# Which engine makes the low halves of the recurrence's split weights: VectorE and GpSimd in turn, or VectorE alone

## What is computed

```python
z = jnp.einsum('bld,de->ble', h, w_in)
x_lru, g_lru, u_s5, gate_a, gate_b = jnp.split(z, SPLITS, axis=-1)
y_a = jax.nn.gelu(g_lru) * rg_lru(causal_depthwise_conv(x_lru, conv_w, conv_b), wa, ba, wx, bx, lam)
y_a = jnp.einsum('blr,rd->bld', y_a, w_lru_out)
y_s = jax.nn.gelu(s5_ssm(u_s5, a_re, a_im, b_re, b_im, c_re, c_im, d, log_dt))
```

## Time and profile before

| | |
|---|---|
| median of 3 runs | 1433.82 us (1431.03 to 1434.45) |
| the profiled execution | 1432.98 us, span 1431.2 us |
| PE busy | 1367.4 us, 96% of the span |
| DVE busy | 968.1 us, 68% |
| ACT busy | 697.3 us, 49% |
| POOL busy | 458.4 us, 32% |
| the four rounds of the recurrence | about 94 to 371 us |

### The profile page before, as it was taken

One profiled execution on the slowest core, in us unless ns is written; L12 is line 12 of the kernel. 1 busy time (PEld: TensorE's weight loads), 2 busy tenths in 40 slices (PEclk: granted clock), 3 DMA queues, 4 the chain that ended last, 5 costly groups with the idle time before them and its releaser, 6 DMA issues.

```text
span 1431.2 us, 19574 instructions
## 1 busy us (share of the span) xinstructions
PE 1367.4 (96%) x6615; PEld 980.0 (68%) x6615; DVE 968.1 (68%) x1429; ACT 697.3 (49%) x994; POOL 458.4 (32%) x361
## 2 busy tenths in 40 slices
PE   7979999999899999999999999999999999999991
PEld 6867778777788888884545666666666666666660
DVE  6788977786511111648626888888778787887875
ACT  4225655647422222210024666676666666676661
POOL 0002432316444444000010433334343355554430
PEclk9989999999999999999999999999999999999996
DMA  9044253534232334741058999999999999999974
GB/s 259 7 128 74 75 75 83 96 63 109 80 100 84 96 104 138 296 169 46 0 202 317 352 367 362 364 365 373 364 371 365 368 371 371 371 366 369 370 226 132
DMA packets 140918, 315.82 MB, mean 221 GB/s; under 512 B 18128, under 2 KB 99712, under 8 KB 115456
## 3 DMA queue, kind: packets, MB, share of 16 engines
q1 hardware_dynamic: 126528, 281.50, 56.5%
q0 software_dynamic: 14336, 33.59, 9.9%
HBM read 297.27 MB, written 34.54 MB: 232 GB/s over the span
## 4 chain that ended last, share of the span: by engine, by line
PE 71%; DMA 11%; DVE 9%; ACT 3%; issue 2%; DVEq 2%; POOL 1%; SPq 1%; ACTq 0%; POOLq 0%
PE bank L723 17%; PE bank L725 16%; PE bank L724 16%; DMA gate_up<-moe_w_up_in 9%; PE bank L1105 5%; PE bank L730 5%; DVE arena L1440 4%; PE bank L892 3%; DVEq L1437 2%; PE bank L970 2%; DVE arena L1446 2%; PE bank L990 1%; ACT arena L1170 1%; ACT gate_up_high L1170 1%; PE bank L1064 1%
## 5 line engine op out<-in xcount | busy, mean ns | idle before, releaser
L1440 DVE TENSOR_TENSOR gate_up_low<-gate_up,gate_up_high 128x1024 fp32r<-128x1024 f32 x256 | 296.6, 1221 | 93.7 <-ACT gate_up_high L1170 93.7
L1170 ACT ACTIVATE gate_up_high<-gate_up 128x1024 fp32r<-128x1024 f32 x256 | 249.7, 1049 | 90.8 <-DMA gate_up<-moe_w_up_in 90.6
L1170 ACT ACTIVATE arena<-bank 96x512 f32<-96x512 f32 (+5 forms) x244 | 128.8, 553 | 250.4 <-PE bank L725 119.2
L672 POOL DMA_INDIRECT acc_dram<-arena x64 | 117.6, 1838 | 317.9 <-DMA acc_dram<-arena 286.1
L723 PE MATMUL bank<-gate_up_high,rows_high 128*96 128x512 f32 x512 | 206.1, 403 | 4.9 <-DVE rows_low L1440 4.9
L1440 DVE TENSOR_TENSOR arena<-arena 128x512 f32<-128x512 f32 (+12 forms) x288 | 194.9, 710 | 15.3 <-ACT arena L1170 3.2
L725 PE MATMUL bank<-gate_up_high,rows_low 128*96 128x512 f32 x512 | 202.6, 396 | 0.0
L724 PE MATMUL bank<-gate_up_low,rows_high 128*96 128x512 f32 x512 | 200.9, 392 | 0.0
L730 PEld LDWEIGHTS bank<-arena 96*128 96x128 f32 (+5 forms) x1001 | 126.5, 186 | 54.1 <-issue 38.2
L599 POOL TENSOR_TENSOR wb_low<-arena,wb_high 128x1024 fp32r<-128x1024 f32 (+1 forms) x40 | 106.7, 2673 | 144.5 <-ACT wb_high L1170 144.5
L730 PE MATMUL bank<-arena 96*128 96x96 f32 (+5 forms) x1001 | 126.6, 265 | 7.9 <-DMA arena<-x_in 4.8
(11 more groups left out here) (171 smaller groups left out, 2586.2 us busy)
## 6 DMA issues: line engine op xcount, KB each, us to landing
gate_up<-moe_w_gate_in SPq DMA_DIRECT2D x64, 1024.0 KB, 18.2
gate_up<-moe_w_up_in SPq DMA_DIRECT2D x64, 1024.0 KB, 21.2
down<-moe_w_down_in SPq DMA_DIRECT2D x64, 1024.0 KB, 16.0
arena<-w_in_in SPq DMA_DIRECT2D x40, 512.0 KB, 4.1
arena<-w_glu_in SPq DMA_DIRECT2D x16, 512.0 KB, 3.9
arena<-w_lru_out_in SPq DMA_DIRECT2D x8, 768.0 KB, 4.7
arena<-x_in SPq DMA_DIRECT2D x8, 512.0 KB, 5.2
wu<-w_in_in SPq DMA_DIRECT2D x8, 512.0 KB, 8.2
```

Of the source, the lines that this page charges most:

```text
L672: nc.gpsimd.indirect_dma_start(out=acc_dram, out_offset=bass.IndirectOffsetOnAxis(ap=idxcol[:, 4 + c:5 + c].bitcast(u32), axis=0), in_=yb[ ...
L1170: return nc.scalar.activation(out_, in_, func, **kw)
L1440: return V_.tensor_tensor(out_, a, b_, op)
```

## The change

Every low part of the x and g weights goes to VectorE. GpSimd loses its twelve (x tiles 0 and 1, g tiles 1 and 2, in three rounds each). On VectorE the low parts of g tiles 1 and 2 stand right behind the convolution of the tile with that number in every round (until now in round 0 only), and those of the next round's x tiles 0, 1 and 2 stand behind `tables_in` (until now tile 2 only). TensorE now waits for them by one count, `v_split`. Waits for `w_split` in the products behind the rounds are renumbered.

```diff
             for b in range(NB):
-                for m in range(1, ML if b else 1):
-                    low_part(wa[m], wa_lo[m], wa_hi[m], ML * (2 * b + 1) + m)
 
                 pool.wait_ge(S["RT_put"], 4 * (b + 1))
                 pool.wait_ge(S["U_put"], 2 * (b + 1))
...
                 pool.sem_inc(S["K_kept"], 1)
-                if b + 1 < NB:
-                    for m in range(2):
-                        low_part(wa[m], wa_lo[m], wa_hi[m], ML * (2 * b + 2) + m)
-                else:
+                if b + 1 == NB:
                     low_b(0)
                     low_b(1)
...
             def x_proj(b, m):
-                if b == 0:
-                    pe.wait_ge(S["v_split"], m + 1)
-                elif m < 2:
-                    pe.wait_ge(S["w_split"], 4 * b + m - 3)
-                else:
-                    pe.wait_ge(S["v_split"], 2 * b + 5)
+                pe.wait_ge(S["v_split"], 2 * ML * b + m + 1)
...
-                    if b == 0:
-                        pe.wait_ge(S["v_split"], ML + m + 1)
-                    elif m == 0:
-                        pe.wait_ge(S["v_split"], 2 * b + 6)
-                    else:
-                        pe.wait_ge(S["w_split"], 4 * b - 2 + m)
+                    pe.wait_ge(S["v_split"], 2 * ML * b + ML + m + 1)
...
                     ins.then_inc(S["conv_done"], 1)
-                    if b == 0 and m:
-                        w_low(m, ML + m)
+                    if m:
+                        w_low(m, ML * (2 * b + 1) + m)
...
                     tables_in(b + 1)
-                    w_low(2, ML * (2 * b + 2) + 2)
+                    for m in range(ML):
+                        w_low(m, ML * (2 * b + 2) + m)
```

More of the change, by code:

```diff
@@ L797, in b_product @@
                 m, j = divmod(v, 5)
-                pe.wait_ge(S["w_split"], 4 * NB - 4 + v + 1)
+                pe.wait_ge(S["w_split"], v + 1)
                 if v == 0:
```

## The result

The changed kernel takes 1437.51 us (median of 20 runs, 1435.67 to 1441.39), the kernel before 1433.68 us (20 runs, 1431.03 to 1436.46). The ratio is 1.0028, 95% interval 1.0021 to 1.0035. The forecast was 1437.7 us, 0.27% more, in a range of 1434.5 to 1440.5. The profiled execution took 1437.79 us with a span of 1435.9 us, 4.7 us longer than before's.

The account below looks back on a forecast made before the run. TensorE, busy 96% of the span, was taken as the bound, so its waits count. Waits of 0.89 + 1.39 + 1.59 = 3.87 us on 1432.98 give 1436.9, or 1437.7 us on the median's footing; range 1434.5 to 1440.5.

Parts of the forecast that it names:

- The place and the kind of loss: At `g_proj(1)` in rounds 1 to 3, TensorE waits for VectorE's low part of g tile 1; 3.87 us in all.
- The step from the start of the convolutions to `g_proj(1)`: On VectorE, six multiply-adds, one low part and the release: 4.71 - 0.08 + 1.22 + 0.10 = 5.95 us.
- The sizes of the waits: Added lateness of `g_proj(1)`: 0.89, 1.39 and 1.59 us in rounds 1, 2, 3; idle times about 2.0, 1.6, 1.8.
- the 0.7 that the prediction gave for both rounds: In rounds 2 and 3, VectorE's convolutions begin 0.7 us before TensorE's K products, hardly moved by the change.
- The relief of 1.5 us: In round 0's tail, VectorE gets 1.5 us ahead without GpSimd's collisions, cutting round 1's lateness from 2.39 to 0.89.
- The single wait for `Q_ready`: Before round 1's K products, TensorE's wait of 1.45 us shrinks to about 0.5, but that gives nothing.
- `K_ready` hidden: Ahead of the S products, `K_ready` comes later but stays covered by the late `g_proj(1)`, with 1.2 us to spare.
- I price the clock at zero: In rounds 1 to 3, new waits of about 1.8 to 2.0 us leave TensorE's clock at 1.00, costing nothing.
- the fall as a rival: The clock falls at each new wait, some 2.9 us each: 1446.4 us, slower by 0.9%; chance 0.04.
- Nothing later gives it back: Behind the rounds, everything starts from TensorE's or its followers' progress, so the 3.87 us lost there stays lost.

Follow-up runs that it names:

- the x and the g tiles alone: Against the kernel before, only the low parts of x tiles 0 and 1 (1431.66 us), or only those of g tiles 1 and 2 (1439.16 us), go to VectorE.
- the kernel with useless work: The changed kernel with six matmuls without use ahead of the wait before `g_proj(1)` in rounds 1 to 3; 1436.86 us, ratio 1.0026.

## Why the prediction was right, point by point

**The place and the kind of loss: right, shown.** All three waits in front of `g_proj(1)` are VectorE's, by its position in the list and not by its load: with the same work one convolution earlier the loss is gone, one later it grows by 2.2 us of waiting a round. The step from the start of the convolutions to `g_proj(1)` was summed to 5.95 us; it is 5.99 in round 1 (176.50 - 170.51) and in round 2 (244.14 - 238.15).

**The sizes of the waits.** The terms were 0.89, 1.39 and 1.59 us. Without falls the rounds grew by 0.7 to 0.8, 1.6 to 1.9 and 1.4 to 2.1 us, 4.0 to 4.5 together, against 3.87. Round 2 was sized too low: the convolutions begin 0.26 us before the K products there (238.15 against 238.41), not 0.69 as before. A wait of ScalarE for the load of g tile 0 ahead of it was 4.49 us against 4.03; that fits, but was not tested. In round 3 the lead of the convolutions differs from trace to trace (305.33 against 306.08 in the first, 303.83 against 303.84 in the third, 300.22 against 300.71 before, so 0.5 us and not the 0.7 that the prediction gave for both rounds), and with it the wait. Over four traces the idle times were 2.2 to 2.3, 1.9 to 2.1 and 1.6 to 2.3 us, where the prediction asked for 2.0, 1.6 and 1.8.

**The relief of 1.5 us: right, shown** by the pair of runs with the x and the g tiles alone. The single wait for `Q_ready` did shrink to 0.45 us.

**`K_ready` hidden: right.** In round 2 it came at 248.07 + 0.41 = 248.48, and TensorE reached the S products at 251.41, later than computed because of the fall. With the waits gone it shows at once, with 0.4 to 1.0 us a round.

**The clock: the step that failed.** The prediction put it so: "I price the clock at zero, and take the fall as a rival", because the new waits seemed far nearer to the one of 1.45 us than to that of 7.37. Over four traces 5 of 12 waits brought a fall at 1.6 us each, 2.0 us a run on average; the rival's price of 2.9 us and its rule of one fall at each wait were both too high. The Trainium skill (TensorE: Matmul & The Clock Gate, section "Why this matters for your kernels") advises against idle gaps over a certain length and would have let these pass; the traces show falls behind waits of 1.9 to 2.4 us, and one behind a wait of 1.12 us, and the measurement decides. Two smaller waits, 0.73 and 0.45 us, lie within 9 us ahead of each of those in the rounds; whether they count was not tested. That waits up to 1.45 us cost nothing, from which the price of zero was argued, held in the rounds and not behind them.

**What came back: not foreseen.** The prediction said "Nothing later gives it back". The kernel before has a fall behind its wait of 2.25 us at 372 us (behind the rounds) in both of its traces, and the changed kernel has none there in four, with a wait of 2.25 to 2.29. The stretch for its first trace and for before's:

```profile
379.50:382.90 3.40, 3.40 (x15) 2.79 (x16) 3.33 (x3) 1.06 (x1) 3.40 (x2) 1.00 0.29 86
```

```profile
373.20:376.60 3.40, 3.40 (x10) 2.65 (x9) 3.33 (x3) 1.06 (x1) 3.40 (x2) 0.51 0.17 49
```

In the same time 15 matmuls are done in place of 10. From this wait to the one near 775 us it is 400.5 to 400.6 us in all four traces of the changed kernel and 402.1 in both of before: the missing fall gives back 1.6 us. So on average the sum is 4.2 (waits) + 2.0 (falls in the rounds) - 1.6 (fall that is missing) + 0.4 (a fall near 779 us in one trace of four) = 5.0, against 3.8 to 4.5 by the medians and 4.2 by the spans of the traces (1435.2 us on average, 1431.0 before). The remaining 0.8 us lies behind the wait near 775 us, where the traces of the changed kernel differ among themselves by up to 2.6 us; its cause is open. The forecast of 3.9 us hit the time partly by luck: terms that it lacked have opposite signs.

Whether the change removes the fall at 372 us is open as well. Over all kernels it came in 4 of 14 traces, at a wait that is nearly the same in all 14 (2.25 to 2.29 us), and in one of two traces of the kernel with useless work, with the same instructions. So the length of the wait does not decide it; that the moment does was not tested, and chance could give two of two against none of four.

## What to carry to other kernels

When work moves to an engine, its busy share says little; look at what stands ahead of the moved instruction in the new list, and at the moment when its reader comes free. Here each place was worth something else: two of the four low parts a round were a gain on the new engine (1.25 us in the rounds, 1.8 by the medians), one cost 0.7 to 2.1 us in each round, and one was hidden. Where a consumer needs a late operand for its last third only, let it start with the rest: that cost nothing and freed the position.

A new wait of about 2 us on TensorE should be priced at its length plus a share of a clock fall (here 5 falls of 1.6 us behind 12 waits), and a time that differs by a few us from run to run may be such falls: compare the same stretch in several traces before explaining it.

## What the runs showed of the hardware that was not expected

- The granted clock fell to its lower level (about 0.5, 1.2 GHz) behind 5 of 12 waits of 1.6 to 2.3 us in the changed kernel, behind 3 of 3 waits of 2.0 to 2.4 us in the one trace with the g tiles alone and behind 3 of 3 waits of 3.9 to 4.5 us. In the rounds of the six traces whose waits are all under 1 us (two of them with the useless matmuls) it never fell. Near 775 us it fell in 4 of 14 traces, behind a wait of 1.12 or 1.13 us. Work without use in the wait, 1.7 us in a gap of about 2, was followed by no fall in six cases.
- A fall of 3.4 us costs 1.6 us of TensorE's time here, in the rounds and behind them (2.6 us for one of 6.8 us). Executions of one kernel differ in how many they have: 2, 1, 0 and 2 in the rounds of four traces.
- A subtraction with both inputs in the on-chip memory on VectorE (0.69 us for 128x512) stretched to 2.68 us beside one of GpSimd, and the six operations of this shape take 4.29 us in place of 6.28 since GpSimd's low part has left. The convolutions, whose first input is a bank of TensorE's memory, last 4.71 us with or without GpSimd's low parts beside them.
